# One core, two blocks of a sequence model: where a norm's inverse root mean square and its shift enter the products

## What is computed

```python
def rms_norm(x, g):
    xf = x.astype(jnp.float32)
    y = xf * lax.rsqrt(jnp.mean(xf * xf, axis=-1, keepdims=True) + EPS)
    return (y * g.astype(jnp.float32)).astype(x.dtype)
...
        h = rms_norm(x, norm_mix[layer]) * (1.0 + scale1) + shift1
...
        x = x + gate1 * y
        h = rms_norm(x, norm_mlp[layer]) * (1.0 + scale2) + shift2
        x = x + gate2 * (jnp.square(jax.nn.relu(h @ mlp_w1[layer])) @ mlp_w2[layer])
```

## Time and profile before

| | us |
|---|---|
| three executions | 1745.07, 1747.36, 1755.98 (median 1747.36) |
| the profiled execution, its own time | 1743.1 |
| its span, first to last instruction | 1741.7 |
| PE (matmul) busy | 1504.5 |
| DVE / ACT / POOL busy | 947.2 / 619.5 / 217.0 |
| mean granted TensorE clock | 0.884 of full speed |

### The profile page before, as it was taken

One profiled execution on the slowest core, in us unless ns is written; L12 is line 12 of the kernel. 1 busy time (PEld: TensorE's weight loads), 2 busy tenths in 40 slices (PEclk: granted clock), 3 DMA queues, 4 the chain that ended last, 5 costly groups with the idle time before them and its releaser, 6 DMA issues.

```text
span 1741.7 us, 27437 instructions
## 1 busy us (share of the span) xinstructions
PE 1504.5 (86%) x12096; PEld 1392.3 (80%) x12096; DVE 947.2 (54%) x1138; ACT 619.5 (36%) x903; POOL 217.0 (12%) x189
## 2 busy tenths in 40 slices
PE   5977589999698687787999777899997899989996
PEld 4976479999696347777999657799985887889996
DVE  3347554545535756999564355555554432455554
ACT  3440243434333234322244104444434432344442
POOL 2000000000000008999620000000000000000000
PEclk7998799999898558898799888999997975999998
DMA  7557246764384012233265003355551420235541
GB/s 292 176 212 280 84 155 232 259 256 179 147 322 171 0 51 97 97 121 121 73 212 187 8 1 121 113 179 192 179 184 50 168 75 0 82 117 189 186 178 73
DMA packets 53815, 253.44 MB, mean 146 GB/s; under 512 B 4096, under 2 KB 4480, under 8 KB 29504
## 3 DMA queue, kind: packets, MB, share of 16 engines
q1 hardware_dynamic: 52272, 245.39, 39.1%
q10 hardware_dynamic: 864, 4.47, 0.7%
q0 software_dynamic: 560, 1.84, 0.4%
HBM read 248.79 MB, written 1.05 MB: 143 GB/s over the span
## 4 chain that ended last, share of the span: by engine, by line
PE 74%; DVE 17%; DMA 4%; ACT 3%; issue 1%; SPq 1%; ACTq 0%; DVEq 0%; POOL 0%
PE PS L335 35%; PE PS L470 19%; DVE w_lo L315 5%; PE PS L333 3%; PE PS L446 2%; PE PS L273 2%; PE PS L1400 2%; DVE arena L870 2%; DVE mlp_lo L528 1%; PE PS L1142 1%; PE PS L748 1%; DVE x_scaled L422 1%; DMA ada_stage<-in_ada 1%; PE PS L1042 1%; DVE mlp_relu L524 1%; PE PS L1407 1%
## 5 line engine op out<-in xcount | busy, mean ns | idle before, releaser
L335 PE MATMUL PS<-act_hi,w_hi 128*128 128x256 f32 x1792 | 529.4, 295 | 99.4 <-DVE w_lo L315 25.1
L315 DVE TENSOR_TENSOR w_lo<-w_stage,w_hi 128x1024 fp32r<-128x1024 f32 x372 | 500.3, 1386 | 180.6 <-ACT w_hi L308 180.1
L335 PE MATMUL PS<-act_lo,w_hi 128*128 128x256 f32 x1792 | 523.0, 292 | 0.0
L335 PE MATMUL PS<-act_hi,w_lo 128*128 128x256 f32 x1792 | 522.3, 291 | 0.0
L335 PEld LDWEIGHTS PS<-act_hi,w_hi 128*128 128x128 f32 x1792 | 360.7, 201 | 109.6 <-issue 38.0
L308 ACT ACTIVATE w_hi<-w_stage 128x1024 fp32r<-128x1024 f32 x372 | 371.5, 1048 | 61.4 <-PE PS L335 40.2
L335 PEld LDWEIGHTS PS<-act_lo,w_hi 128*128 128x128 f32 x1792 | 360.9, 201 | 0.0
L335 PEld LDWEIGHTS PS<-act_hi,w_lo 128*128 128x128 f32 x1792 | 360.3, 201 | 0.0
L470 PE MATMUL PS<-mlp_hi,w_hi 128*128 128x256 f32 x1024 | 289.2, 282 | 13.9 <-DVE w_lo L315 7.9
L470 PE MATMUL PS<-mlp_lo,w_hi 128*128 128x256 f32 x1024 | 288.3, 282 | 0.0
L470 PE MATMUL PS<-mlp_hi,w_lo 128*128 128x256 f32 x1024 | 288.1, 281 | 0.0
(11 more groups left out here) (284 smaller groups left out, 1583.9 us busy)
## 6 DMA issues: line engine op xcount, KB each, us to landing
w_stage<-in_w SPq DMA_DIRECT2D x186, 1024.0 KB, 4.8
ada_stage<-in_ada SPq DMA_DIRECT2D x27, 1024.0 KB, 8.0
x_scaled<-in_ada SPq DMA_DIRECT2D x13, 1024.0 KB, 8.5
arena<-in_ada SPq DMA_DIRECT2D x8, 1024.0 KB, 14.9
arena<-in_ssm_in ACTq DMA_DIRECT2D x1, 2048.0 KB, 9.1
x_res<-in_x ACTq DMA_DIRECT2D x1, 1024.0 KB, 6.4
out<-x_scaled ACTq DMA_DIRECT2D x1, 1024.0 KB, 3.9
x_scaled<-ada_stage POOLq DMA_DIRECT2D x1, 448.0 KB, 3.4
```

The source lines that it names most:

```text
L315: vec.tensor_tensor(wlo[s][:, c], stage[s][:, c], whi[s][:, c].bitcast(F32), ALU.subtract).then_inc(*w_lo.mark(q, h))
L335: m = pe.matmul(o, w[:, k, c], a[:, k, :], start=first, stop=last)
```

## The change

- **No normalised tensor in front of the products.** act_hi and act_lo are now taken from x times the norm's weights g, tile by tile: act_hi = round(x·g) on ACT, act_lo = x·g − act_hi on DVE, one instruction each per tile. x_scaled is no longer written there.
- **rstd behind the products.** It is one number per token, and a product is linear, so each result is multiplied by it where it leaves PSUM, on DVE: `evacuate` in the MLPs, `vec_scaled` (keys and queries of fox), `vec_qkv`. Values of fox are token-major and take it as ACT's scale, from two transposed columns (`rcol`). For the values of layer 1 the full act_hi and act_lo are still made, late, under the products of the keys.
- **The shift as columns.** Where a norm has a shift (MLP 0, MLP 1, q and k of layer 1), `act_hi` and `act_lo` are 258 columns wide: column 256 holds the shift, 257 zero. The product's column 256 is then shift·W; it is read into `small` (`shift_out`) and added on ACT as a bias. An up product then needs two banks.
- **The sum of squares** runs in the middle of the first gemm: after its first output tile 8 products onto 32 partitions each (`pe_strips`), then after the second, one product that adds the four strips (`pe_sum`).
- **Earlier release.** `h_free` tells ACT, tile by tile, that the last gemm of a phase has read act_hi, so the next phase's tile is written under it.
- **Squaring moves to ACT** in the MLPs (relu and square; square alone without a shift), the PSUM read to DVE.
- **The forget gates** leave the head of norm 6 and stand behind the second key gemm; POOL makes their x·g.
- **SP's waits** for the norms go, but for one; the modulation columns move to another bank; the final output leaves in four DMAs instead of one; pe_ssm_taps takes turns on two banks instead of three.

```diff
-        hh = sb("act_hi", [P, KT, S], F32R)
-        hl = sb("act_lo", [P, KT, S], F32R)
+        hh_wide = sb("act_hi", [P, KT, S + 2], F32R)
+        hl_wide = sb("act_lo", [P, KT, S + 2], F32R)
+        hh, hl = hh_wide[:, :, 0:S], hl_wide[:, :, 0:S]
...
-                    if n % 3 == 2:
-                        sp.wait_ge(*vec_norm.at(ADA_BEHIND[g], "lo", KT - 2))
+                    if n == 2:
+                        sp.wait_ge(*vec_norm.at(0, "lo", KT - 2))
...
+                    if t == 1 and free and k < KT - 1:
+                        m.then_inc(*h_free.mark(q, k))
+                if t == 1:
+                    m.then_inc(*w_used.mark(q))
+                if norm is not None:
+                    (pe_strips, pe_sum)[t](norm)
...
+        def act_tile_hi(j, k, g, behind=None):
+            act.wait_ge(*vec_norm.at(j, "x", k))
+            if behind is not None:
+                act_wait_free(behind, k)
+            act.activation(hh[:, k, :], x[:, k, :], ACT.Copy, scale=g[:, k:k + 1]).then_inc(
+                *act_norm.mark(j, "hi", k))
+
+        def vec_tile_lo(j, k, g):
+            vec.wait_ge(*act_norm.at(j, "hi", k))
+            vec.scalar_tensor_tensor(hl[:, k, :], x[:, k, :], g[:, k:k + 1], hh[:, k, :].bitcast(F32),
+                                     ALU.mult, ALU.subtract).then_inc(*vec_norm.mark(j, "lo", k))
...
+        def pe_strips(j):
+            b = SUM_BANK[j] * 512
+            for k in range(KT):
+                a = k % 4
+                pe.wait_ge(*act_norm.at(j, "sq", k))
+                m = pe.matmul(PS[32 * a:32 * a + 32, b:b + S], ones[:, 0:32], SQUARES[j][:, k, :], start=k < 4,
+                              stop=k >= 4, skip_group_check=True, tile_position=(0, 32 * a))
+            m.then_inc(*pe_norm.mark(j, "strips"))
...
+            def square(c):
+                act.wait_ge(*vec_mlp.at(l, c, "evacuated"))
+                if l < 2:
+                    for t in range(2):
+                        a = act_a[:, t * S:(t + 1) * S]
+                        m = act.activation(a, a, ACT.Relu, bias=shift_out(c)[:, t:t + 1])
+                    m.then_inc(*act_mlp.mark(l, c, "relu"))
+                    act.wait_ge(*act_mlp.last())
+                act.activation(act_a[:], act_a[:], ACT.Square).then_inc(*act_mlp.mark(l, c, "squared"))
...
+            def evacuate(q, c):
+                vec.wait_ge(*w_used.at(q))
+                if c:
+                    vec.wait_ge(*vec_mlp.at(l, c - 1, "lo"))
+                if l < 2:
+                    b = up_bank(l, c, 0)[0] * 512 + S
+                    vec.tensor_copy(shift_out(c), PS[:, b:b + 513:512])
+                    m = vec.tensor_tensor(a2, up_view(l, c), rstd2, ALU.mult)
+                else:
+                    m = vec.scalar_tensor_tensor(a2, up_view(l, c), 0.0, rstd2, ALU.max, ALU.mult)
+                m.then_inc(*vec_mlp.mark(l, c, "evacuated"))
...
+            for n in range(KT + 2):
+                if n < KT:
+                    vec.scalar_tensor_tensor(x[:, n, :], PS[:, n * S:(n + 1) * S],
+                                             gate[:, n:n + 1] if gate is not None else one[:],
+                                             x[:, n, :], ALU.mult, ALU.add).then_inc(*vec_norm.mark(j, "x", n))
+                if n >= 2 and g is not None:
+                    vec_tile_lo(j, n - 2, g)
...
-            pe_norm_program(6)
-            pe.wait_ge(*vec_norm.at(6, "normed", KT - 2))
-            pe_gates()
-            pe_gemm(Q_K2, 4, act_out, norm=6)
...
+            pe_gemm(Q_K2, 4, vec_out.at, lo_of=lo_of(6), norm=6, after={1: pe_gates})
```

More of the change, by code:

```diff
@@ L439, in pe_norm_program @@
-        def pe_norm_program(j, sq=squares0):
-            for k in range(0, KT, 2):
-                if k % 4:
-                    pe.wait_ge(*vec_norm.at(j, "sq", k))
-                else:
-                    pe.wait_ge(*act_norm.at(j, "sq", k))
-                for t in (k, k + 1):
-                    m = pe.matmul(PS[:, 7 * 512:7 * 512 + S], ones[:], sq[:, t, :], start=t == 0, stop=t == KT - 1)
-            m.then_inc(*pe_norm.mark(j))
-        def pe_mlp(l, groups=None, between=None):
+        rstd2 = rstd[:].unsqueeze(1).to_broadcast([P, 2, S])
@@ L459, in down, with out_of @@
+                width = S + 2 if l < 2 else S
+                def out_of(t):
+                    b, o = up_bank(l, c, t)
+                    return PS[:, b * 512 + o:b * 512 + o + width]
+                pe_up(q, out_of, wide=l < 2, lo_of=None if c else lo_of(j),
+                      norm=None if c else j)
             def down(q, c):
@@ L1480, in vec_fox, with pe_first_norm @@
                     vec_pair_lo("fox", (step - 4) // 2)
+        def pe_first_norm():
+            for k in range(0, KT, 2):
+                if k % 4:
+                    pe.wait_ge(*vec_norm.at(0, "sq", k))
+                else:
+                    pe.wait_ge(*act_norm.at(0, "sq", k))
+                for t in (k, k + 1):
+                    m = pe.matmul(PS[:, 7 * 512:7 * 512 + S], ones[:], squares0[:, t, :], start=t == 0,
+                                  stop=t == KT - 1)
+            m.then_inc(*pe_norm.mark(0))
         def act_first_norm():
```

571 lines of the change are left out of this document (348 added, 223 removed).

## The result

Four executions of the changed kernel took 1627.47, 1662.11, 1657.69 and 1645.62 us, median 1651.65, beside a median of 1746.21 for the kernel before. The ratio is 0.937, with a 95% interval of 0.931 to 0.943, so the kernel is faster by 5.8 to 6.9%. The profiled execution is the fastest of the four, 1627.47 us with a span of 1626.1, against 1743.1 and 1741.7 before: 115.6 us less, where I had counted 82.7. The other three took 18 to 35 us longer than it. Up to 23 us of that can lie in one place, the largest thing that I had not looked at; the rest stays unexplained, since those executions have no profile.

The account below looks back on a forecast made before the run. PE, busy 1504.5 us, bounds the kernel, with about 150 us of norms to gain from. Savings of 84.3 less 1.6 for wider gemms, 82.7, take 1743.1 to 1660.4; the median stands 4.3 higher: 1665 us, range 1638 to 1702.

Parts of the forecast that it names:

- nine stretches that end at a norm: Stretches where PE mostly waits or runs at the lower clock: 208.7 us together, about 150 of them norm.
- Norms 1, 4, 5, 7, 8: Priced step by step from profile rows: savings of 9.4, 4.1, 10.6, 10.1 and 4.2 us.
- Norms 6 and 9: Norm 6 with later gates saves 10.5 us, between 6 and 15; norm 9, under the last value gemm, 7.6.
- Norm 2: Norm behind MLP 0: 16.2 us in place of 27.9, 11.7 saved.
- the chunk's wait: At norm 2, 7.11 us for a weight chunk queued on SP behind an ada load; it goes.
- Norm 3 and MLP 1: Norm 3 saves 9.6 us, MLP 1's pairs under POOL 7.5, between −20 and +15.
- the taps: Taps at the end of POOL's work in MLP 1: two banks cost 1 us.
- the one more turn of GpSimd's: In MLP 1's pairs w_hi waits 2.65 us for DVE's input, so another POOL turn passes: 16.2 us, not 14.3.
- POOL's own list: In MLP 1, it must end before the taps are used; it holds the +15 us case, 14.3 a pair.
- The clock: Rival: at seven hand-overs before gemms the clock falls, up to 4.5 us each, 30 us lost, 1695; chance 0.12.
- Moved chains: Rival: dearer steps before down(0); norms give 50 of 70, MLPs take 25 back, 1710 us; chance 0.14.
- Rows off their grid: Rival: 1032-byte act_hi rows slow PE's 5376 products; at 30 ns each 161 us lost, 1826; chance 0.04.

Follow-up runs that it names:

- the filling: 48 unused full-width products put after the fifth step of the forgetting attention, in the kernel before (median 1738.4 us) and in the changed kernel (median 1637.1 us).
- the run with SyncE's waits: Changed kernel with SyncE again waiting for the norm before later loads of the adaptation weights: 1649.32 us.
- the run with ACT's order changed: Changed kernel, but in MLP 0 and 1 ACT makes the next chunk's rounded half before the second activation's square: median 1634.33 us.
- norm 7 in full: Changed kernel with norm 7 alone done in the old order, ahead of the products: 1636.96 us in one execution.
- the filling ahead of the scores: Changed kernel with 40 unused full-width products before the stick-breaking attention's scores, and 48 before its third head: median 1631.6 us.

## Why the prediction was right or wrong

**Direction and size.** Faster was forecast, at 1665 us within 1638 to 1702. The median of the changed kernel, 1651.65, lies inside; the ratio, which sets it at 0.931 to 0.943 of 1746.2, puts it at 1625 to 1646, at and below the low end, and the profiled execution, at 1627.47, lies below it.

**The step that failed** is a sentence that is not there, the one that would have said why all outside the norms stays as long as it was. "Nothing in the change removes one of these", I wrote of the products, "What is left are nine stretches that end at a norm", and cut the kernel into norms and the rest; the rest was taken as constant. Both attentions were in that rest with PE at half its clock. I had read the granted clock at the norms only. In the forgetting attention 88.6 us became 65.6 in the profiled executions, with not one of its products changed, and this 23.0, which the sum has at nothing, is 70% of the 33 us by which it fell short. How much of it belongs to the change is only partly answered. Unfilled, the kernel before had its attention at 87.3 us from first to last product in both its profiles, the changed kernel at 64.4 in six of seven (78.2 in the other), so the change does seem to favour the good case where a profile is taken; but the unprofiled executions of the changed kernel took 18 to 35 us longer, and why the clock comes back early or late stays open. Without the attention the first pair of profiles differs by 92.6 us. The pair in which both have the filling differs by 100 to 101 us (medians 1738.4 and 1637.1, profiled 1735.57 and 1635.63), 1.5 of them in the attention. So what the change does outside the attention is worth 93 to 99 us, against the 82.7 forecast, and the rest of the 115.6 is the attention's clock.

**Norms 1, 4, 5, 7, 8** were right within 1 us each: 8.7, 3.9, 9.9, 10.0 and 5.0 for 9.4, 4.1, 10.6, 10.1 and 4.2. The priced steps hold singly too: strips 1.00 for 1.1, sum 0.45 for 0.5, out of PSUM 0.77 for 0.9, up to down(0) at 17.06 for 17.0.

**Norms 6 and 9**, 25.0 for 18.1, were mis-sized mostly in one term. For the other three key gemms I added the gates' 4.3, stalls of 3.7 and 1 for POOL on top of the 20.0 us that they took before, which makes 29. But these 20.0 already held 2.7 of a clock at 0.86, behind a pause of 4.72. Now they are at 1.00, the gates' products take 3.63 + 0.44, the two pauses 1.66 and 1.2, and the whole 24.2:

```profile
1268.73 3.63 PE L1546 MATMUL PS<-x_scaled,arena 128*16 128x256 f32 x16
1272.29 0.44 PE L1550 MATMUL PS<-ident,rstd 128*128 128x128 f32 x2
1287.34 0.39 PE L338 MATMUL PS<-w_hi,act_hi 128*128 128x256 f32 x1 [1.66 <-DVE w_lo L319]
```

The head of norm 6 took 12.1 where I had 14, since its half-idle first half did not bring the lower clock.

**Norm 2**, 14.5 for 11.7, errs the same way: I took 16.2 us, from a strips-and-second-half of 4.0 at the full or 6.5 at the lower clock, and it took 13.6 at 1.00. That the chunk's wait would go was right, and the run with SyncE's waits shows it to be 7.5 us.

**Norm 3 and MLP 1**, 15.0 for 17.1, and the taps, −3.6 for −1: the one more turn of GpSimd's was placed rightly, behind the 2.65 us wait for w_hi (2.59 measured), and the run with ACT's order changed shows it. The pair is 16.8 for 16.2. The stretch took 185 to 197 us in the five profiles of the kernel before and its variants, so its 15.0 is good to some us at best. The taps lost 3.6, which I had put at 1: 2.4 because each group of transposes waits for the copy out of its bank (12.2 in place of 9.8 us), and about 1.1 because the first group now waits for the copy of the taps. That POOL's own list would hold the stretch at about 14.3 us a pair stood in the range, and with ACT's order changed, at 14.9, it does.

**The start and MLP 0.** The first stretch takes 118.5 to 120.4 us in nine profiles of this kernel and its variants, and 120.4 to 122.1 in five of the kernel before and its variants: they differ by about 2 us on average, and why stays open. The 4.2 of the recurrent mixer is mostly scatter: 82.4 to 87.4 us before, 81.5 to 88.5 after. MLP 0 lost 1.0 us in five profiles and 2.5 in the four with the cold down(0).

**The rivals.** *The clock*: refuted as a cost of 30 us. In the first profile all hand-overs are at 1.00 but for one down(0), 1.7 us. It is not gone altogether: in the profiles with ACT's order changed and with norm 7 in full the clock was down for 6.8 us at norm 2, and norm 2 with its gemms took 89.8 us in place of 88.4. *Moved chains*: up's and down's sets keep their pace, MLP 2 and 3 at 173.5 and MLP 0 at +1.0 or +2.5. *Rows off their grid*: refuted, 172.02 us for 1440 products against 171.97. The prediction's estimate from the Trainium skill (SBUF — State Buffer, the row on cachelines in Specifications (TRN2)) was 5 us on 5376 products that read act_hi or act_lo. The 720 of them in MLP 2 would have 0.7, and 0.05 was measured; the measurement decides. The Trainium skill's rule in the section Who interferes with whom of the same page agrees: under POOL the instruction out of PSUM takes 0.68 us, against 0.61 without, and the w_lo halves with two SBUF operands 2.4 to 3.2, against 1.2.

## What to carry to other kernels

Moving a norm's scale behind the products takes its chain off PE's path. That part can be priced from the rows, stretch by stretch: to within a microsecond for five of the norms here, and 2 to 7 us off where a clock or a stall had to be guessed. Read the granted clock over the whole span and not only where the change is: a stretch in which PE is always busy and the clock is at half is worth more than most edits, and some dozens of unused full-array products in it can pay for themselves. When one engine's wait is taken out of a stretch shared with a long list on another, look first at when that list ends, since it sets how much of the gain stays.

## What the runs showed of the hardware

TensorE was busy without a gap and was granted 1.2 GHz all the same, for 71.6 us on end in the forgetting attention, where 192 of 304 products use part of the array. 48 products on 64x64 cells left the clock at 0.50; 48 on 128x128 in float32r, or 12 in float32, were followed by 1.00 to the attention's end (attention 96.2 against 73.8 and 73.5 us). 128x128 products of 16 columns each had the clock at 0.50 too, 16.2 us busy of 16.2. The same attention with the same instructions took 64.4, 78.2 or 87.3 us from first to last product. With the filling the spread of the changed kernel's four executions fell from 2% to 0.6%, so a good part of it is this clock; other stretches vary too, and what decides when the clock comes back without the wide products stays open. The Trainium skill (TensorE: Matmul & The Clock Gate, Part 1, The HAM clock gate) lets the clock follow how busy PE has been. That agrees with the cold down(0) behind a pause of 2.02 us, and not with the forgetting attention, 71.60 us busy of 71.60 at clock 0.50, if busy is what the profile counts; the measurement decides. In the stick-breaking attention the filling ahead of the scores ended at 557.8 us, the scores began at 560.7, and the clock was down again from 561.2.
